# A hybrid decoder layer on one core: the front projections in three passes of rounded parts, the convolution's sums in PSUM, and a new tile order

## The chip, the cores and the metric

The kernel runs on one core of a Trainium2 chip. The metric is the device time of one execution in microseconds (us). In the text PE is TensorE (matrix products), DVE is VectorE, ACT is ScalarE, POOL is GpSimd and SP is SyncE, which here only issues transfers.

## The reference, cut to what matters

One layer for 256 prompt tokens and 8 sequences of 4 sample tokens, 288 tokens in all, with D_MODEL 1024:

```
h   = RMSNorm(x) * (1 + scale1) + shift1          # scale, shift, gate from silu(c) @ w_ada
h @ w_in -> q, k, v, indexer q, indexer k, indexer weights, conv input (a, g), gates A and B
branch A: the indexer picks top-k keys; softmax attention over them; @ w_o_attn
branch B: z = a * sigmoid(g); causal depthwise conv, width 31; LayerNorm; silu; @ w_conv_out
x += gate1 * ((sigmoid(gA) * A + sigmoid(gB) * B) @ w_out)
x += gate2 * PEER(RMSNorm(x) * (1 + scale2) + shift2)     # 16384 experts
```

The change lies in the front: `h @ w_in` without the gates, and the convolution. Everything from `w_conv_out` on keeps its products.

## The kernel before, in words

Activations are kept transposed: 128 channels on the partitions, 8 chunks `k`, 288 tokens along a row. A weight tile is 128x1024 float32 (512 KB) and gives 128 output channels for all tokens. SP streams the tiles in the order of `LOADS` through a ring of four slots: load n is issued when tile n-4 is done. `POS[key]` is a tile's place in that order, which `PLAN` sets by hand.

- The start: 16 `ada` tiles (four groups, `FIRST`) give scale1 and shift1. After two groups PE turns them (`mod_turned` 1), after all four again (`mod_turned` 2). DVE then makes `hT`, ACT and POOL make its rounded part and its remainder (`rhs_parts`, "h2r" in the profile).
- `HEAD`: 31 tiles (8 `conv_a`, 8 `conv_g`, `ki`, 4 `qi`, 2 `k`, 8 `q`), three `v` pieces whose weights lie in `v_w`, and 16 later `ada` tiles, one after each two of the others. `linear` (L1476) multiplies a tile straight from the ring as float32: 8 products that the profile shows as 16 records. ACT copies each result out of one of two PSUM banks `lin` (`evac`, or the sigmoid of L697). Beside that ACT loads the 16 pages of the key caches, two after each `conv_g` (`load_page`, L684).
- A tile of a stage in `STAGES` is cut instead (`CUT` is their list): ACT writes its part rounded to float32r (`cut_tile`, L667), POOL subtracts to get the remainder (`low_tiles`, L561), both into `split`, which has two slots; PE then does three passes of 8 products (`linear_cut`, L1513, L1519, L1525): high x high, high x low, low x high.
- The convolution is DVE's. For a pair of chunks it makes `z` (L1010, L1012), then 31 taps for each chunk by turns (L1019, L1023): 2 + 60 instructions of 128x256. The running sums stand in `y`, in SBUF. `conv_a` of chunk k goes to PSUM bank `pa[k % 4]`, so chunk k+4 waits for the `z` of chunk k. After the four pairs come the sample tokens: four times a product (L1033) and a reduction (L1036) of 128x1984, the "sample taps".
- The index stage (`for n in range(NQ * IH)`, 16 turns) follows the head: each second turn a `gate_a` tile and an `ada` tile, each turn an indexer head (PE L1633, relu L748 on ACT, L1063 on DVE), and from turn 3 on the QK norm's spread (L1641, L1070). Between them lie the LayerNorm's sums over `y` (L1457, after turn 6, waits for `y_sample`), the subtraction of the mean (L1076), ACT's square and the second sums (L1457, turn 12). Then come the sample indexer products (L1652), and a chain of DVE work (the top-k) up to the attention.

## Time and profile before

| | |
|---|---|
| median of 3 runs | 1407.49 us (1406.44 to 1407.97) |
| the profiled execution | 1407.39 us, its span 1405.6 us |
| PE busy | 1337.5 us (95%) |
| DVE, ACT, POOL busy | 976.6, 592.3, 767.8 us (69%, 42%, 55%) |
| mean granted TensorE clock | 0.976 |

The span is first to last instruction; 1.8 us of the time lie around it. A PE that is busy in 95% of the span counts the modelled ends of its instructions as well. A granted clock of 1.00 is 2.4 GHz and 0.50 is 1.2 GHz.

### The profile page before, as it was taken

What the parts mean: (1) busy time and instruction counts of PE and PEld (TensorE: products, weight loads), DVE (VectorE), ACT (ScalarE), POOL (GpSimd) and SP (SyncE); (2) the same over time, 40 slices, a digit from 0 to 9 for tenths busy, and PEclk for the clock granted to TensorE, in tenths of its full rate; (3) what the DMA queues carried; (4) which work ended last, traced back from release to release, by engine and by line L of the source; (5) the groups of instructions that cost most, each with busy time, mean ns of one, the idle gap of its engine ahead of it and who ended that gap; (6) DMA issues with size and microseconds to landing.
All of it is one profiled execution on the core that took longest, in us unless ns stands there. A gap on an engine that the chain in (4) does not pass through costs nothing.

```text
span 1405.6 us, 30010 instructions
## 1 busy us (share of the span) xinstructions
PE 1337.5 (95%) x9976; PEld 1253.2 (89%) x9976; DVE 976.6 (69%) x2130; ACT 592.3 (42%) x932; POOL 767.8 (55%) x335
## 2 busy tenths in 40 slices
PE   5999999889989999799999999999999999999996
PEld 3777677767879999789999999999999999999996
DVE  2499923965435999992666565650788888888886
ACT  1200234355434444554444444444444444444442
POOL 0200023520655477786655556557777777777774
PEclk8999999889998999999999999999999999999998
DMA  8776454234443456455545545456666666666663
GB/s 315 275 244 204 146 201 160 89 126 139 147 158 106 136 180 207 145 176 192 168 159 166 168 162 168 159 166 223 220 211 210 210 210 211 212 211 212 215 211 134
DMA packets 103750, 258.37 MB, mean 184 GB/s; under 512 B 12496, under 2 KB 52144, under 8 KB 103312
## 3 DMA queue, kind: packets, MB, share of 16 engines
q1 hardware_dynamic: 94144, 245.81, 52.0%
q10 hardware_dynamic: 8752, 8.93, 1.9%
q0 software_dynamic: 800, 2.91, 0.6%
q8 instruction: 33, 0.54, 0.2%
q14 instruction: 21, 0.17, 0.0%
HBM read 234.60 MB, written 23.00 MB: 183 GB/s over the span
## 4 chain that ended last, share of the span: by engine, by line
PE 87%; DVE 4%; issue 3%; POOL 2%; DMA 2%; ACT 1%; ACTq 0%; SPq 0%; POOLq 0%; DVEq 0%
PE ps L1868 28%; PE ps L1821 9%; PE ps L1476 9%; PE ps L1814 9%; PE ps L1815 8%; PE ps L1849 5%; PE ps L1513 4%; PE ps L1519 4%; PE ps L1525 3%; POOL split L596 2%; DMA ring<-in_stream 2%; PE ps L1536 1%; PE ps L1457 1%; PE ps L1799 1%; PE ps L1596 1%
## 5 line engine op out<-in xcount | busy, mean ns | idle before, releaser
L596 POOL TENSOR_TENSOR split<-ring,split 128x1024 fp32r<-128x1024 f32 x256 | 629.5, 2461 | 274.2 <-ACT split L869 274.0
L1868 PE MATMUL ps<-h2r,split 128*128 128x288 f32 x3072 | 406.4, 294 | 0.9 <-ACT h2r L931 0.9
L1868 PEld LDWEIGHTS ps<-h2r,split 128*128 128x128 f32 x3072 | 406.2, 188 | 1.1 <-ACT x L898 1.1
L869 ACT ACTIVATE split<-ring 128x1024 fp32r<-128x1024 f32 x256 | 270.4, 1057 | 205.7 <-PE ps L1868 204.1
L1436 DVE TENSOR_TENSOR h2r<-x,h2r 128x288 fp32r<-128x288 f32 x128 | 298.8, 2335 | 76.5 <-ACT h2r L931 76.5
L1814 PE MATMUL ps<-h2r,split 128*128 128x288 f32 x1024 | 284.9, 305 | 5.2 <-ACT split L869 5.2
L1815 PE MATMUL ps<-h2r,split 128*128 128x288 f32 x1024 | 278.8, 296 | 0.0
L561 POOL TENSOR_TENSOR split<-ring,split 128x1024 fp32r<-128x1024 f32 x48 | 118.7, 2475 | 179.1 <-ACT split L667 179.0
L1814 PEld LDWEIGHTS ps<-h2r,split 128*128 128x128 f32 x1024 | 193.9, 189 | 5.8 <-ACT split L869 3.8
L1815 PEld LDWEIGHTS ps<-h2r,split 128*128 128x128 f32 x1024 | 193.5, 189 | 0.0
L1821 PE MATMUL ps<-h2r,split 128*128 128x288 f32 x1024 | 165.3, 304 | 6.7 <-POOL split L596 6.4
L1821 PEld LDWEIGHTS ps<-h2r,split 128*128 128x128 f32 x1024 | 142.6, 190 | 9.8 <-POOL split L596 9.8
L898 ACT ACTIVATE x<-ps 128x288 f32<-128x288 f32 x124 | 51.1, 412 | 238.0 <-PE ps L1821 236.0
L1404 DVE TENSOR_SCALAR x<-ps,x 128x128 f32<-128x128 f32 x144 | 49.8, 346 | 117.3 <-PE ps L1849 107.2
L1476 PE MATMUL ps<-big,ring 128*128 128x288 f32 x496 | 127.2, 414 | 1.7 <-ACT mod L651 1.7
L1476 PEld LDWEIGHTS ps<-big,ring 128*128 128x128 f32 x496 | 93.5, 192 | 31.5 <-ACT big L657 2.9
L1405 DVE TENSOR_SCALAR x<-ps,x 128x128 f32<-128x128 f32 x288 | 115.5, 401 | 0.0
L1023 DVE SCALAR_TENSOR_TENSOR big<-big 128x256 f32<-128x256 f32 x240 | 95.3, 478 | 0.0
L1513 PE MATMUL ps<-h2r,split 128*128 128x288 f32 x448 | 79.6, 319 | 14.1 <-ACT split L667 5.5
L1513 PEld LDWEIGHTS ps<-h2r,split 128*128 128x128 f32 x448 | 66.8, 197 | 24.4 <-issue 16.4
L1519 PE MATMUL ps<-h2r,split 128*128 128x288 f32 x448 | 76.1, 309 | 0.0
L1427 DVE TENSOR_TENSOR x<-x,big 128x288 f32<-128x288 f32 x128 | 59.0, 461 | 20.3 <-DMA x<-act_dram 20.2
(240 smaller groups left out, 1349.1 us busy)
## 6 DMA issues: line engine op xcount, KB each, us to landing
ring<-in_stream SPq DMA_DIRECT2D x391, 512.0 KB, 3.3
act_dram<-x SPq DMA_DIRECT2D x128, 144.0 KB, 1.8
x<-act_dram SPq DMA_DIRECT2D x128, 144.0 KB, 3.0
big<-in_cache_k ACTq DMA_DIRECT2D x16, 128.0 KB, 3.3
big<-in_cache_v ACTq DMA_DIRECT2D x16, 128.0 KB, 3.2
x<-in_xT ACTq DMA_DIRECT2D x1, 1152.0 KB, 7.9
x_dram<-x ACTq DMA_DIRECT2D x1, 1152.0 KB, 5.2
big<-x_dram SPq DMA_DIRECT2D x1, 1152.0 KB, 5.0
```

The source lines that it names most:

```text
L561: nc.gpsimd.tensor_tensor(split[:, n % 2, 1], ring[:, POS[key] % R, :], split[:, n % 2, 0].bitcast(f32), ALU.subtract).then_inc(lin_lo, 1)
L596: nc.gpsimd.tensor_tensor(split[:, n % 2, 1], ring[:, slot_of(n), :], split[:, n % 2, 0].bitcast(f32), ALU.subtract).then_inc(lo_ready, 1)
L869: nc.scalar.activation(split[:, n % 2, 0], ring[:, slot_of(n), :], ACT.Copy).then_inc(hi_ready, 1)
L1405: return V.tensor_scalar(hot1[slot], iota_ps, parts[:, 0, col], parts[:, 2, col], ALU.is_equal, ALU.mult)
L1436: V.tensor_tensor(wr[:, n % 2, 1], act_b[:, n], wr[:, n % 2, 0].bitcast(f32), ALU.subtract)\
L1476: last = MM(bank[:, 0:T], w[:, k], rhs[:, k], start=(k == 0), stop=(k == KC - 1))
L1513: MM(out, hi[:, k], h_hi[:, k], start=(k == 0), stop=False)
L1519: last = MM(out, hi[:, k], h_lo[:, k], start=False, stop=False)
L1814: MM(out, u_hi[:, k], h_hi[:, k], start=(k == 0), stop=False)
L1815: last = MM(out, u_hi[:, k], h_lo[:, k], start=False, stop=False)
L1821: last = MM(out, u_lo[:, k], h_hi[:, k], start=False, stop=(k == KC - 1))
L1868: ins = MM(ps[k][:, 0:T], v[v_part][:, k], wr[:, n % 2, w_part], start=start, stop=stop)
```

## The change

- `STAGES[0]` takes the head's 31 tiles in: they are cut by ACT and POOL and multiplied by `linear_cut` in three passes; `linear` is gone. `rhs_lo` of `hT` is made in 8 chunks on POOL, and POOL cuts the head's remainders before it stores the convolution's state.
- The taps' running sums stand in the PSUM bank `pa[3]`; only the last tap writes `y`. `conv_a` has three banks left (`NCONV`).
- `HEAD`'s order: `ki` and `qi` after four chunks of the convolution, `v` and `k` before the last two chunks.
- Page loads move from ACT to SP: one page after each second tile load from load 24 on.
- `v_w`, `dist`, `causal` are issued at `mod_turned` 1 in place of 2.
- The sample taps move from behind the convolution into turns 1, 3, 5, 7 of the index stage; the sums over `y` move from turn 6 to 10, the subtraction from 7 to 11, the second sums from 12 to 14, ACT's `root(3)` behind the loop.

```diff
-HEAD = LINEAR[:LINEAR.index(("gate_a", 0))]
...
+HEAD = (CONV[:8] + [("ki", 0)] + [("qi", n) for n in range(4)] + CONV[8:12] + [("v", t) for t in range(NT)]
+        + [("k", n) for n in range(KV)] + CONV[12:] + [("q", n) for n in range(H)])
+NCONV = 3
...
-STAGES = [("gate_a", "gate_b"), ("conv_out",), ("attn_out",), ("out",), ("peer_q",)]
+STAGES = [("conv_a", "conv_g", "ki", "qi", "k", "q", "gate_a", "gate_b"), ("conv_out",), ("attn_out",), ("out",), ("peer_q",)]
...
+PAGES_AT = 24
...
+                page = (n - PAGES_AT) // 2
+                if n >= PAGES_AT and (n - PAGES_AT) % 2 == 0 and page < NSEQ * NPAGES:
+                    if page == 0:
+                        sp.wait_ge(pages_in, 16)
+                    load_page(page)
...
-            pool.wait_ge(mod_turned, 2)
+            pool.wait_ge(mod_turned, 1)
...
+            for k in range(KC):
+                pool.wait_ge(rhs_hi, k + 1)
+                nc.gpsimd.tensor_tensor(rhs_parts[:, 1, k * T:(k + 1) * T], hT[:, k],
+                                        rhs_parts[:, 0, k * T:(k + 1) * T].bitcast(f32), ALU.subtract).then_inc(rhs_lo, 1)
...
+            low_tiles(STAGES[0][:-2])
+            pool.wait_ge(conv_staged, 2)
...
+            cut_tile(CUT[0])
             cut_rhs(hT, h_ready, 3)
...
             for key in HEAD:
                 kind, m = key[:2]
+                if key in CUT:
+                    cut_tile(CUT[CUT.index(key) + 1])
...
-                        yp, w = y[:, k, 0:TP], wdw[:, k, j:j + 1]
+                        yp, w = pa[NCONV][:, k % 2 * TP:(k % 2 + 1) * TP], wdw[:, k, j:j + 1]
...
-                            ins = V.scalar_tensor_tensor(yp, zp[:, k, j:j + TP], w, yp, ALU.mult, ALU.add)
+                            ins = V.scalar_tensor_tensor(yp if j < CW - 1 else y[:, k, 0:TP], zp[:, k, j:j + TP], w, yp,
+                                                         ALU.mult, ALU.add)
...
-                if n == 7:
+                if n % 2 and n < 2 * TD:
+                    sample_taps(n // 2)
...
+                if n == 11:
...
-                    linear(key, hT, h_ready if key == ("conv_a", 0) else None)
+                    linear_cut(key)
...
-                if n == 6:
+                if n == 10:
```

SP's queue from its first row on, in the difference of the two programs. `ring<-in_stream` is a tile load, `pages` and `in_cache_...` belong to a page; the second page's rows repeat the first's.

```order
-L464 DMA ring<-in_stream 128x1024 x89
...
+L464 DMA ring<-in_stream 128x1024 x25
+L467 TENSOR_LOAD pages
+L467 ISA x2
+L470 ISA
+L470 DMA big<-in_cache_i 64x128 x2
+L470 ISA
+L470 DMA big<-in_cache_k 128x256
+L470 DMA big<-in_cache_v 128x256
+L464 DMA ring<-in_stream 128x1024 x2
```

Before, 89 tile loads stood in a row; now a page's rows stand behind load 24 and then behind each second load, sixteen times.

DVE before, from the last pair's taps to the first turns of the index stage (`big` holds `zp`, `y` and most other arrays, `ps` is PSUM):

```order
L1023 SCALAR_TENSOR_TENSOR big<-big 128x256 x60
L1033 TENSOR_TENSOR big<-big 128x1984
L1036 TENSOR_REDUCE big<-big 128x8x8
...
L1038 TENSOR_TENSOR big<-big 128x8x32
L1042 RECIPROCAL big<-big 10x288
L1049 TENSOR_TENSOR big<-big,ident 32x128 x2
L1060 TENSOR_SCALAR big<-big 128x128
```

And the same place now:

```order
L1024 SCALAR_TENSOR_TENSOR ps<-big,ps 128x256 x58
L1024 SCALAR_TENSOR_TENSOR big<-big,ps 128x256 x2
L1032 RECIPROCAL big<-big 10x288
L1053 TENSOR_SCALAR big<-big 128x128
L1056 SCALAR_TENSOR_TENSOR big<-big 128x128
L1040 TENSOR_TENSOR big<-big 128x1984
L1043 TENSOR_REDUCE big<-big 128x8x8
L1056 SCALAR_TENSOR_TENSOR big<-big 128x128 x2
L1063 SCALAR_TENSOR_TENSOR big<-big,ps 128x288
L1040 TENSOR_TENSOR big<-big 128x1984
L1043 TENSOR_REDUCE big<-big 128x8x8
```

The sample taps (a product and a reduction) stood ahead of the reciprocal and stand now inside the turns; the taps read and write PSUM.

POOL before, behind its first memsets, and then the same place now:

```order
L541 DMA big<-in_v_w 128x8x264
L546 TENSOR_TENSOR h2r<-big,h2r 128x2304
L550 DMA out_convpT<-big 128x240
L551 DMA out_convsT<-big 128x1920
L561 TENSOR_TENSOR split<-ring,split 128x1024 x8
```

```order
L552 DMA big<-in_v_w 128x8x264
L558 TENSOR_TENSOR h2r<-big,h2r 128x288 x8
L569 TENSOR_TENSOR split<-ring,split 128x1024 x31
L574 DMA out_convpT<-big 128x240
L575 DMA out_convsT<-big 128x1920
L569 TENSOR_TENSOR split<-ring,split 128x1024 x8
```

The one subtraction for `hT` became eight, and 31 remainders of head tiles stand behind them.

## Rows read from the trace of the kernel before

**Rows 1.** Two of the page's costliest groups: busy us, mean ns of one.

```profile
L869 ACT ACTIVATE split<-ring 128x1024 fp32r<-128x1024 f32 x256 | 270.4, 1057 | 205.7 <-PE ps L1868 204.1
...
L1023 DVE SCALAR_TENSOR_TENSOR big<-big 128x256 f32<-128x256 f32 x240 | 95.3, 478 | 0.0
```

**Rows 2.** The chain that ended last, the head's begin: start us, us, what.

```profile
38.92 9.14 PE ps L1476 x32
...
48.63 7.96 PE ps L1476 x32
```

**Rows 3.** The same chain where the head ends and a cut tile begins.

```profile
191.70 1.25 PE ps L1513 x8
...
195.07 0.57 PE ps L1536 x16
```

**Rows 4.** The same chain in the attn_out stage, cut tiles one after another.

```profile
363.06 1.07 PE ps L1513 x8
...
366.26 1.07 PE ps L1513 x8
```

**Rows 5.** Timeline in the head: start us, us, engine, line, operation, idle before.

```profile
97.22 0.99 PE L1476 MATMUL ps<-big,ring 128*128 128x288 f32 x3 [1.73 <-ACT mod L651]
```

**Rows 6.** Lines' own answers, POOL: duration ns min/median/max, first and last start.

```profile
L575 POOL TENSOR_TENSOR h2r<-big,h2r x8: 791/837/1007, 285.5 to 291.3; 128x288 fp32r<-128x288 f32 x8
...
L561 POOL TENSOR_TENSOR split<-ring,split x48: 2338/2397/4726, 188.2 to 484.2; 128x1024 fp32r<-128x1024 f32 x48
```

**Rows 7.** Timeline: PE turns two groups.

```profile
22.15 0.41 PE L1571 MATMUL ps<-ident,big 128*128 128x128 f32 x2 [1.04 <-ACT big L637]
```

**Rows 8.** Windows: us, busy of PE, PEld, DVE, ACT, POOL, granted clock, DMA share, GB/s.

```profile
24.00:36.00 12.00, 7.58 (x112) 4.30 (x112) 5.10 (x23) 0.28 (x1) 0.00 (x0) 0.52 0.99 381
```

**Rows 9.** Transfers issued from 40 to 192 us: KB each, median us to landing.

```profile
ring<-in_stream SPq DMA_DIRECT2D x47, 512.0 KB, 4.0
...
big<-in_v_w POOLq DMA_DIRECT2D x1, 1056.0 KB, 6.2
```

**Rows 10.** Timeline: two pages in a row on ACT's queue.

```profile
49.02 1.21 ACTq L684 DMA_DIRECT2D big<-in_cache_i  x2
...
52.08 1.13 ACTq L684 DMA_DIRECT2D big<-in_cache_i  x2
```

**Rows 11.** Timeline, DVE: the first sample taps, a product and a reduction.

```profile
158.25 2.22 DVE L1033 TENSOR_TENSOR big<-big 128x1984 f32<-128x1984 f32 x1
...
160.51 2.22 DVE L1036 TENSOR_REDUCE big<-big 128x64 f32<-128x1984 f32 x1
```

**Rows 12.** Timeline, the index stage: a DVE instruction beside POOL's.

```profile
201.06 2.38 POOL L561 TENSOR_TENSOR split<-ring,split 128x1024 fp32r<-128x1024 f32 x1 [5.79 <-ACT split L667]
...
201.58 2.47 DVE L1063 SCALAR_TENSOR_TENSOR big<-big 128x128 f32<-128x128 f32 x2 [0.63 <-ACT big L748]
```

**Rows 13.** Timeline, the out stage: DVE beside POOL, with PSUM operands.

```profile
392.50 0.48 DVE L1263 SCALAR_TENSOR_TENSOR x<-ps,mod,x 128x256 f32<-128x256 f32 x1 [2.38 <-PE ps L1525]
392.55 2.41 POOL L561 TENSOR_TENSOR split<-ring,split 128x1024 fp32r<-128x1024 f32 x1 [0.79 <-ACT split L667]
392.91 0.19 DVE L1265 TENSOR_TENSOR ps<-ps,mod 128x32 f32<-128x32 f32 x1
```

**Rows 14.** Lines' own answers, the index stage on DVE: ns min/median/max.

```profile
L1063 DVE SCALAR_TENSOR_TENSOR big<-big x14: 342/480/2010, 200.6 to 243.5; 128x128 f32<-128x128 f32 x7, 128x256 f32<-128x256 f32 x7
...
L1070 DVE SCALAR_TENSOR_TENSOR big<-big,ps x10: 499/505/514, 204.0 to 238.1; 128x288 f32<-128x288 f32 x10
```

**Rows 15.** Timeline, the index stage: DVE, ACT and PE.

```profile
198.01 1.94 DVE L1042 RECIPROCAL big<-big 10x288 f32<-10x288 f32 x1 [21.28 <-ACT big L726]
...
218.07 3.99 DVE L1076 TENSOR_TENSOR big<-big 128x2304 f32<-128x2304 f32 x1
...
222.10 2.13 ACT L615 ACTIVATE big<-big 128x2304 f32<-128x2304 f32 x1 [0.17 <-DVE big L1076]
...
243.21 4.17 PE L1652 MATMUL ps<-big 64*128 64x16 f32 x64 [0.74 <-ACT big L748]
```

More of the change, by code:

```diff
@@ L83, in spread @@
     return out
-HEAD = LINEAR[:LINEAR.index(("gate_a", 0))]
-HEAD.insert(HEAD.index(("k", 0)), ("v", 0))
-for t in range(1, NT):
-    HEAD.insert(HEAD.index(("v", t - 1)) + 1, ("v", t))
+HEAD = (CONV[:8] + [("ki", 0)] + [("qi", n) for n in range(4)] + CONV[8:12] + [("v", t) for t in range(NT)]
+        + [("k", n) for n in range(KV)] + CONV[12:] + [("q", n) for n in range(H)])
+NCONV = 3
 HEAD = spread(HEAD, 0, 16, 2)
@@ L464, in load, with load_page @@
                 sp.dma_start(ring[:, slot, :], a["stream"][n]).then_inc(tile_loaded[slot], 16)
+            def load_page(n):
+                page = sp.value_load(pages[0:1, n:n + 1], min_val=0, max_val=a["cache_k"].shape[0] - 1)
+                for dst, src in ((cache_i[0:ID, n], "cache_i"), (cache_i[ID:P, n], "cache_i"),
+                                 (cache_k[:, n].rearrange("p v n -> p (v n)"), "cache_k"), (cache_v[:, n], "cache_v")):
+                    sp.dma_start(dst, a[src][bass.ds(page, 1)].rearrange("o p n -> (o p) n")).then_inc(cache_in, 16)
             for n, at in enumerate(LOADS):
@@ L711, in _ @@
                 else:
-                    n = QK.index(key)
-                    if n == len(QK) - 1:
-                        cut_tile(("gate_a", 0))
                     evac(key, kT[:, m] if kind == "k" else q[:, m])
-                    evac(key, sq_qk[n], ACT.Square)
+                    evac(key, sq_qk[QK.index(key)], ACT.Square)
                     if key == ("q", 3):
@@ L749, in _ @@
                     .then_inc(idx_relu, 1)
+            root(3)
             eng.wait_ge(s_idx_prod, 1)
@@ L1027, in _, with sample_taps @@
                             ins.then_inc(y_prompt, 1)
+            dve.wait_ge(qk_root, 1)
+            V.reciprocal(qk_rms[0:len(QK)], qk_rms[0:len(QK)]).then_inc(qk_rstd, 1)
             samples = y[:, :, TP:T].rearrange("p k (b t) -> p k b t", t=TD)
-            for t in range(TD):
+            def sample_taps(t):
                 settle()
@@ L1076, in _ @@
                     V.tensor_tensor(y[:, :, :], y[:, :, :], over_chunks(rstd), ALU.subtract).then_inc(y_centred, 1)
+            dve.wait_ge(y_prompt, KC)
+            dve.wait_ge(y_sample, 1)
+            dve.wait_ge(conv_stored, 32)
+            wi = vtok[0:TS, NQ, KV * P:VW].rearrange("p (pair par) -> p par pair", par=2)
+            for par in range(2):
+                V.tensor_tensor(wi_diag[0:TS, par * 4:par * 4 + 4], wi[:, par].unsqueeze(2).to_broadcast([TS, 4, TS]),
+                                ident[0:TS, 0:TS].unsqueeze(1).to_broadcast([TS, 4, TS]), ALU.mult).then_inc(s_wi, 1)
             dve.wait_ge(idx_used, NQ * IH)
@@ L1458, in sums @@
                 return last
-            def linear(key, rhs, chunk_ready=None):
-                if key[0] == "conv_a":
-                    bank = pa[key[1] % 4]
-                    if key[1] >= 4:
-                        pe.wait_ge(z_ready, 2 * (key[1] - 4) + 2)
-                else:
-                    bank = lin[BANK[key]]
-                    free(BANKED.index(key))
-                pe.wait_ge(tile_loaded[POS[key] % R], 16 * (POS[key] // R + 1))
-                w = ring[:, POS[key] % R, :].rearrange("p (k m) -> p k m", m=P)
-                for k in range(KC):
-                    if chunk_ready is not None:
-                        pe.wait_ge(chunk_ready, 3 * k + 3)
-                    last = MM(bank[:, 0:T], w[:, k], rhs[:, k], start=(k == 0), stop=(k == KC - 1))
-                last.then_inc(tile_done, 1)
             def free(n):
@@ L1505, in linear_cut @@
                     if half == 0:
-                        free(BANKED.index(key))
+                        if key[0] == "conv_a":
+                            if key[1] >= NCONV:
+                                pe.wait_ge(z_ready, 2 * (key[1] - NCONV) + 2)
+                        else:
+                            free(BANKED.index(key))
                         pe.wait_ge(lin_hi, n + 1)
```

48 lines of the change are left out of this document (13 added, 35 removed).

## The prediction

> **What bounds the kernel now.** From the page I took that PE is busy in 95% of the span, so I looked at what the PE does in the front and at who would have to keep up with a faster PE. The chain that ended last runs through L1476, tile after tile, from 38.9 to 191.7 us [rows 2, 3]: the head is bound by PE. Two float32 tiles take 7.96 us [rows 2], 3.98 each, and with the ada tile behind them, 0.57 [rows 3], a pair takes 8.53. In all of it PE waited once, 1.73 us, for an ACT that was issuing page loads [rows 5]. Before the head PE waits for tile loads: from 24 to 36 us the DMA engines are 99% busy at 381 GB/s, and the granted clock is 0.52, near the 1.2 GHz level, while PE has gaps [rows 8]. Behind the head the index stage runs from 191.7 to the start of L1652 at 243.2 [rows 3, 15], 51.5 us, with a PE that hardly waits. The convolution ends on DVE at 158.3 and the sample taps follow it [rows 11], both hidden under the head.
>
> **The tiles: gain.** A cut tile that begins after other work takes from 191.70 to 195.07, 3.37 us [rows 3]; in a row they take 3.20 each [rows 4]. A head pair would be 3.37 + 3.20 + 0.57 = 7.14 us against 8.53: 0.70 us for each tile, and 31 tiles give **-21.7**. The page loads leave ACT, so its stall goes: **-1.7** [rows 5]. Bounds: -18 if each tile took 3.37 and the stall came back elsewhere, -24 if each took 3.20. ACT's cut of 1.06 [rows 1] and POOL's remainder of 2.40 [rows 6] come to 2.1 and 4.8 us in a pair of 7.14, so the PE covers them once they run ahead of it.
>
> **The first tiles: loss.** Float32 products needed only `hT`. Now ACT first cuts tile 0, then the 8 chunks of `hT`, and POOL makes 8 remainders of 0.84 us, as in L575 [rows 6], 6.7 in all. With the first chunk at about 39.5 they end at 46.2, tile 0's remainder at 48.6, its last pass (1.07 [rows 4]) at 49.7; tile 1's remainder at 51.0, PE at 52.1, ada at 52.7; tile 2's at 53.4, PE at 56.1; tile 3's cut stands on ACT behind the sigmoid of tile 1, so its remainder comes at 56.0, PE at 59.3, ada at 59.9. Before, that point was 57.2 [rows 2], and at the new pace it would be 54.4. The ramp costs **+5.5**. Bounds +4 (POOL a fifth quicker) and +9 (PE, with gaps, stays at the low clock through two tiles).
>
> **`v_w` earlier: loss.** `v_w`, `dist` and `causal` are 1056 [rows 9] + 128 + 128 KB, 1.34 MB. They used to start with `mod_turned` 2, when the head begins. Now they start at 22.6 [rows 7], into the stretch in which the DMA engines are full and PE waits for each tile. At 381 GB/s [rows 8] 1.34 MB are 3.5 us, by which the last ada tile, and the whole head, comes later: **+3.5**. Bounds 0 and +4.
>
> **Pages on SP: loss.** One page is 3.06 us of issuing on ACT's queue (49.02 to 52.08) [rows 10]; no row shows it on SP, and I take the same. Load n is issued when tile n-4 is done and lands 4.0 us later [rows 9]. Between lie 7.14 us, of which the cut wants 1.06: 2.1 to spare. Where a page follows the load of an ada tile, the next load is due 0.57 us later and is issued some 2.9 late, about 0.9 beyond what is spare. With pages behind each second load this comes once in six loads, five times in 32, less by slack at the `v` pieces: three to four times 0.9, **+3**. Bounds 0 (loads land in 3 us) and +8.
>
> **The convolution: nothing, by cover.** A DVE instruction with two SBUF inputs waits while POOL runs: at 201.58 two L1063 took 2.47 us, until POOL's of 201.06 had ended [rows 12]. With 31 remainders in the head the old form would meet that all along. With the sums in PSUM one SBUF tensor is left, and L1265 (one PSUM and one SBUF input, PSUM output) began 0.36 us into POOL's 2.41 and took 0.19 [rows 13]. Its length: 240 taps fill 95.3 us, 0.397 apart and 478 ns long [rows 1]; the nearest with a PSUM input and a pointer scalar, L1263, is 0.48 long [rows 13], so 0 to 0.02 more for each. It begins at 59.3 + 3.5 + 0.5 = 63.3, needs some 26 us for each of four pairs, waits for the late last `conv_g` at some 147 us, and ends near 174. It is wanted by the reciprocal of L1042, 6.3 us behind the head's end [rows 15], which is near 187 now. So 13 us are spare; spacing decides only above 0.49 us a tap.
>
> The Trainium skill, "VectorE: DVE Perf Modes", section "The TRN2 errata — SBUF-src ops pay a fixed extra latency per instruction", gives VectorE a fixed 120 cycles from PSUM against 58 from SBUF. By that estimate a tap would be 0.065 us longer (15.6 us over 240) and the convolution would end some 12 us later than I have it, just covered; the rows here show a fifth of that or less.
>
> **Sample taps in the index stage: loss.** They are 2.22 + 2.22 us four times [rows 11], 18 us that the head hid. In turns 1 to 7 DVE has for each two turns 4.5 of taps and some 1.6 of its own (two L1063, two L1070 [rows 14]), and the product has two SBUF inputs, so it collides with POOL's remainders, say 0.5 each: 6.6 us. PE has (51.5 less two sums of 4.0) / 8 = 5.4, and it waits for DVE through the spread (`qk_ready`), two turns behind. Four rounds: 4 x 1.2 = 4.8. The subtraction and the square, 4.0 + 2.1 [rows 15], now have only turns 11 to 14 over them in place of 7 to 12: 0.7 more. PE's lead of two turns gives back about half a round, 2.5. **+3**. Bounds 0 and +8 (each collision in full, 2.4). `root(3)` and `wi_diag` fill waits of ACT and DVE under L1652's 4.2 us [rows 15]; what follows is unchanged.
>
> **Sum.** -21.7 - 1.7 + 5.5 + 3.5 + 3 + 3 = -8.4. Against the profiled execution's own 1407.4 us, which is the median within 0.1, that is **1399.0 us**. Under 0.2% (2.8 us, so above 1404.7) is about what can't be told from no change.
>
> **The rivals.**
> *The losses are covered.* SP issues a page more quickly or loads land in 3 us, and the taps find more room than I see: then ramp and `v_w` alone count, -14.4: 1393.0; with `v_w` hidden too, 1389.5. For it: DVE is idle between the convolution's end and the first turns. Against: 6.6 us in two turns are plain sums of rows. Chance 0.22.
> *The clock eats the gain.* In the ramp and the index stage PE gets gaps, and it had 0.52 where it had gaps before [rows 8]. Four tiles at 1.2 GHz would be 13 us longer, half of it under waits already counted: -8.4 + 6.5, 1405.5. Against: at 191.7 a pass still took 1.07 us as in the full stream [rows 4]. Chance 0.13.
> *SP becomes the bound* (the slower side). Two loads want 0.8 us of SP and PE takes 4.8 for two loads. Above 4.0 us a page SP sets the pace, and each microsecond more costs 16. At 4.5 the gain is gone (+8); at 4.9 it is -8.4 + 14.4 = +6, 1413.4. For it: no row shows a page on SP. Against: 3.06 on ACT [rows 10]. Chance 0.10.
> *The taps wait for POOL after all.* Pointer scalar and chunk both lie in SBUF; if that counts as two inputs, 31 remainders of 2.4 us block DVE for 74 us, the convolution ends near 248, 61 beyond its cover: 1460. Against: [rows 13]. Chance 0.04.
>
> **How the numbers follow.** The forecast holds 0.51; its own range, by half of the bounds, is 1394 to 1404. The range over all takes in the covered case and most of the clock's: **1389 to 1407**; SP's bound and the blocked taps lie outside. Faster by over 0.2%: 0.51 x 0.98 + 0.22 + 0.13 x 0.25 = 0.75. Within: the rest of the clock's case and the edges, 0.11. Slower: 0.10 + 0.04 = 0.14.
>
> **What would show it.** Cut tiles of 3.2 to 3.4 us in the head; the head's first product near 42.4 instead of 38.9; the fourth tile done near 63 instead of 56.6; waits of ACT or PE in the head for `ring`, three to five of about 0.9 us; the head's end near 180; taps 0.40 to 0.42 apart; an index stage of 54 to 55 us in which PE waits for DVE. I am wrong if the start doesn't move, if SP's queue has no waits for tiles left (SP bound), if taps stand over 0.49 apart, or if the granted clock is near 0.50 behind 50 us.

## The result: no gain, 0.27% slower

The changed kernel took 1411.2 us (median of 12 runs, 1406.11 to 1414.61) against 1407.2 us (12 runs, 1404.97 to 1409.85): ratio 1.0027, 95% interval 1.0015 to 1.0038. The forecast was 1399.0 us; the time lies outside the range and on the other side of no change. Where a number below is "before" without a group, it is from the trace of the kernel before.

The page of the changed kernel, whose profiled execution took 1412.23 us:

```profile
span 1410.4 us, 30634 instructions
...
PE 1330.5 (94%) x10224; PEld 1271.4 (90%) x10224; DVE 983.6 (70%) x2130; ACT 623.1 (44%) x963; POOL 844.8 (60%) x373
```

PE is 7.0 us less busy than before, and the span is 4.8 us longer: the products did become cheaper, and gaps took 11.8 us, more than they saved. Read at five points of the two traces (us from the span's start):

| | before | changed | difference | forecast |
|---|---|---|---|---|
| head's first product | 38.7 | 42.3 | +3.6 | +3.5 |
| fifth tile starts | 57.1 | 65.0 | +7.9 | +6.3 |
| head's end | 191.7 | 186.8 | -4.9 | -11.4 |
| sample indexer products | 243.2 | 244.0 | +0.8 | -8.4 |
| span | 1405.6 | 1410.4 | +4.8 | -8.4 |

The first row is the start in the timeline of both kernels; the 38.9 of the prediction is the same product in the chain of [rows 2].

**The head's begin.** Timelines of PE (start us, us, engine, line, operation, idle before), the second turning of the `ada` results in the kernel before and in the changed one, then the first cut product:

```profile
38.26 0.66 PE L1571 MATMUL ps<-ident,big 128*128 128x128 f32 x2 [0.49 <-ACT big L637]
```

```profile
40.19 0.66 PE L1565 MATMUL ps<-ident,big 128*128 128x128 f32 x2 [0.49 <-ACT big L649]
```

```profile
42.26 1.85 PE L1507 MATMUL ps<-h2r,split 128*128 128x288 f32 x5 [1.40 <-ACT h2r L686]
```

The first turning began at 22.15 before [rows 7] and begins at 21.91 now, so between the two lie 18.3 us in place of 16.1: the `ada` tiles come 2.2 us later behind the earlier `v_w`. From the second turning to the first product it is 2.07 us in place of 0.45, because a cut product also waits for ACT's rounded `hT`.

The chain that ended last (start us, us, what), where [rows 2] show the kernel before:

```profile
49.14 2.34 POOL split L569
...
51.52 2.29 PE ps L1519 x8
53.81 1.49 PE ps L1507 x8
...
57.38 0.57 PE ps L1530 x16
```

POOL's remainder of tile 0 is ready at 51.5, 0.6 earlier than summed (48.6 + 3.5). But the pass that waits for it takes 2.29 us in place of 1.07, and the next 1.49. The windows say why (columns as in [rows 8]):

```profile
40.00:50.00 10.00, 5.41 (x16) 3.98 (x17) 6.82 (x16) 5.84 (x12) 7.20 (x9) 0.50 0.35 126
50.00:60.00 10.00, 9.32 (x68) 8.61 (x68) 0.52 (x2) 4.61 (x5) 7.33 (x4) 0.77 0.30 97
```

PE was busy 5.4 of the 10 us from 40 on, with gaps, and the granted clock stood at 0.50, the 1.2 GHz level; before, with PE busy without a gap, it was 0.92 there. The first two tiles end 1.8 us later than summed.

DVE and POOL in the same stretch (timelines):

```profile
41.67 0.41 DVE L999 TENSOR_SCALAR big<-big,scl,mod 128x256 f32<-128x256 f32 x1
...
42.20 0.95 DVE L999 TENSOR_SCALAR big<-big,scl,mod 128x256 f32<-128x256 f32 x1
...
43.79 0.83 DVE L998 TENSOR_TENSOR big<-big,scl 128x32 f32<-128x32 f32 x1
```

```profile
42.20 5.54 POOL L558 TENSOR_TENSOR h2r<-big,h2r 128x288 fp32r<-128x288 f32 x7 [17.55 <-ACT h2r L686]
```

As soon as POOL begins its remainders of `hT`, DVE's instructions that write the next chunks of `hT` take two to five times as long (before: 0.40 and 0.18). I had only thought of ACT and POOL there.

**The middle of the head.** The chain where the SP queue issues a page; L464 is a tile's load, L467 the page number's register, L470 the page's transfers:

```profile
68.44 3.83 DMA ring<-in_stream
...
79.33 1.08 PE ps L1519 x8
...
80.43 0.34 SPq L464
...
80.81 0.27 SPq L467
...
84.05 0.38 SPq L470
...
84.48 3.99 DMA ring<-in_stream
...
88.49 1.06 ACT split L679
...
89.69 1.29 PE ps L1507 x8
...
99.99 5.08 DMA ring<-in_stream
```

A tile is done at 80.41 and one load is issued; behind it stands a page, from 80.81 to 84.43 (3.6 us). The next load is due at 80.97, when the `ada` tile is done, and is issued only at 84.48. It lands 3.99 later, is cut in 1.06, and PE starts at 89.69, having waited 0.86. Such a load comes once in six, as forecast: those of 68.44, 84.48 and 99.99 are issued 3.3, 3.5 and 2.7 us late (forecast 2.9). The page shown is one of the long ones. The sixteen pages on SP take 2.93 to 3.97 us each in this trace, median 2.94, so the price taken, 3.06, was right. PE by lines from 65 to 122 us (last column: idle before, and for whom):

```profile
L1507 PE MATMUL ps<-h2r,split 128*128 128x288 f32 x104 | 16.5, 301 | 4.2 <-ACT split L679 3.7 <-ACT big L669 0.5
```

Seven pairs with their `ada` tiles lie between 65.03 and 121.68, 8.09 us each, not 7.14 (one of the fourteen is a `v` piece). In stretches of two pairs, each with one late load: from 65.03 to 81.33, to 97.81 and to 113.71 it is 16.30, 16.48 and 15.90 us, where e3 below takes 14.30 (72.56 to 86.86). A late load thus costs 1.6 to 2.2 us, though PE's wait for it is 0.86 to 1.24, as forecast: the pair behind it waits as well (0.36 at 81.33, 0.53 at 97.81).

**The index stage.** Chain at the head's end, then timelines of DVE, POOL and PE; before: [rows 3, 11, 12, 15]:

```profile
186.79 1.26 PE ps L1507 x8
...
193.12 1.92 DVE big L1032
```

```profile
197.99 2.22 DVE L1043 TENSOR_REDUCE big<-big 128x64 f32<-128x1984 f32 x1
200.13 3.02 DVE L1056 SCALAR_TENSOR_TENSOR big<-big 128x128 f32<-128x128 f32 x2
```

```profile
196.16 6.38 POOL L569 TENSOR_TENSOR split<-ring,split 128x1024 fp32r<-128x1024 f32 x2 [5.79 <-ACT split L679]
```

```profile
244.00 2.20 PE L1646 MATMUL ps<-big 64*128 64x16 f32 x34 [0.74 <-ACT big L748]
```

Two remainders of 2.4 us take 6.38 beside DVE's sample taps, and DVE's L1056 then 3.02 for two (before 0.35 each where POOL was idle). From 186.8 to 244.0 the stage takes 57.2 us against 51.5. PE waits only 2.0 us in it:

```profile
L1519 PE MATMUL ps<-h2r,split 128*128 128x288 f32 x66 | 10.8, 305 | 1.1 <-POOL split L569 1.1
...
L1635 PE MATMUL ps<-big,ident 10*128 10x288 f32 x20 | 6.9, 439 | 0.9 <-DVE big L1063 0.9
```

In this trace the rest is in the passes: in this stretch, by the same view, one record of L1507 and L1513 takes 328 and 332 ns, and of the same two passes before (L1513, L1519) 308 and 295; the granted clock was 0.83, 0.92 and 0.90 in the three stretches of 10 us from 200 on, and 1.00 in all of them before. But the lower clock is not what makes the stage long. e3 (below) has the same code in this stage; its windows row:

```profile
180.40:237.00 56.60, 51.57 (x409) 40.40 (x408) 37.65 (x37) 21.82 (x42) 22.82 (x12) 1.00 0.51 182
```

With the clock at 1.00 throughout, its stage takes 56.6 us all the same. PE waits 4.3 us in it in place of 2.0, and DVE is busy for 37.7 us as in the changed kernel, against 19.4 before. So the work on DVE sets the length (e10 takes part of it away), and PE spends the time in waits or in slow passes.

**The convolution.** DVE's timeline, 58 taps of a pair:

```profile
66.54 22.81 DVE L1024 SCALAR_TENSOR_TENSOR ps<-big,ps 128x256 f32<-128x256 f32 x58
```

22.81 / 58 is 0.393 us a tap, beside a POOL that cuts a tile every 3.5 us; before it was 0.397 [rows 1] with POOL idle.

### The profile page after: what moved, and what is told of

The parts are those of the page before. It is cut to its first block, busy times and chain, and to the rows that moved or that the text cites. A ratio compares the mean times of both kernels' runs of the same rounds, so it can differ in the third digit from the quotient of the medians.

```text
span 1410.4 us, 30634 instructions
## 1 busy us (share of the span) xinstructions
PE 1330.5 (94%) x10224; PEld 1271.4 (90%) x10224; DVE 983.6 (70%) x2130; ACT 623.1 (44%) x963; POOL 844.8 (60%) x373
## 4 chain that ended last, share of the span: by engine, by line
PE 81%; DVE 6%; issue 4%; DMA 4%; POOL 2%; ACT 2%; SPq 1%; POOLq 0%; ACTq 0%; DVEq 0%
PE ps L1862 28%; PE ps L1815 9%; PE ps L1808 8%; PE ps L1809 8%; PE ps L1507 6%; PE ps L1513 5%; PE ps L1519 5%; PE ps L1843 5%; DMA ring<-in_stream 3%; POOL split L608 2%; PE ps L1530 1%; PE ps L1465 1%; PE ps L1793 1%; DVE big L1132 1%; PE ps L1590 1%
## 5 line engine op out<-in xcount | busy, mean ns | idle before, releaser
L608 POOL TENSOR_TENSOR split<-ring,split 128x1024 fp32r<-128x1024 f32 x256 | 628.9, 2458 | 273.8 <-ACT split L870 273.7
L1862 PE MATMUL ps<-h2r,split 128*128 128x288 f32 x3072 | 406.4, 294 | 0.9 <-ACT h2r L932 0.9
L1862 PEld LDWEIGHTS ps<-h2r,split 128*128 128x128 f32 x3072 | 406.2, 188 | 1.1 <-ACT x L899 1.1
L870 ACT ACTIVATE split<-ring 128x1024 fp32r<-128x1024 f32 x256 | 270.4, 1056 | 205.8 <-PE ps L1862 202.7
L569 POOL TENSOR_TENSOR split<-ring,split 128x1024 fp32r<-128x1024 f32 x79 | 194.1, 2464 | 234.1 <-ACT split L679 221.7
L1808 PE MATMUL ps<-h2r,split 128*128 128x288 f32 x1024 | 285.1, 306 | 5.2 <-ACT split L870 5.2
L1809 PE MATMUL ps<-h2r,split 128*128 128x288 f32 x1024 | 278.7, 296 | 0.0
L1808 PEld LDWEIGHTS ps<-h2r,split 128*128 128x128 f32 x1024 | 194.0, 189 | 5.8 <-ACT split L870 3.8
L1809 PEld LDWEIGHTS ps<-h2r,split 128*128 128x128 f32 x1024 | 193.7, 189 | 0.0
L1815 PE MATMUL ps<-h2r,split 128*128 128x288 f32 x1024 | 164.9, 303 | 5.6 <-POOL split L608 5.2
L1815 PEld LDWEIGHTS ps<-h2r,split 128*128 128x128 f32 x1024 | 142.3, 189 | 8.9 <-POOL split L608 8.9
L1507 PE MATMUL ps<-h2r,split 128*128 128x288 f32 x696 | 124.7, 322 | 23.7 <-ACT split L679 10.2
L1507 PEld LDWEIGHTS ps<-h2r,split 128*128 128x128 f32 x696 | 105.0, 200 | 40.6 <-issue 23.7
L1412 DVE TENSOR_SCALAR x<-ps,x 128x128 f32<-128x128 f32 x144 | 49.8, 346 | 113.9 <-PE ps L1843 107.2
L679 ACT ACTIVATE split<-ring 128x1024 fp32r<-128x1024 f32 x87 | 91.8, 1055 | 83.0 <-DMA ring<-in_stream 56.4
L1513 PE MATMUL ps<-h2r,split 128*128 128x288 f32 x696 | 118.5, 314 | 0.0
L1519 PE MATMUL ps<-h2r,split 128*128 128x288 f32 x696 | 111.2, 303 | 1.9 <-POOL split L569 1.8
L1513 PEld LDWEIGHTS ps<-h2r,split 128*128 128x128 f32 x696 | 106.2, 202 | 1.6 <-DVE h2r L1244 0.2
L1519 PEld LDWEIGHTS ps<-h2r,split 128*128 128x128 f32 x696 | 101.3, 196 | 3.8 <-POOL split L569 3.7
```

What stands on the lines that cost most here:

```text
L569: nc.gpsimd.tensor_tensor(split[:, n % 2, 1], ring[:, POS[key] % R, :], split[:, n % 2, 0].bitcast(f32), ALU.subtract).then_inc(lin_lo, 1)
L608: nc.gpsimd.tensor_tensor(split[:, n % 2, 1], ring[:, slot_of(n), :], split[:, n % 2, 0].bitcast(f32), ALU.subtract).then_inc(lo_ready, 1)
L870: nc.scalar.activation(split[:, n % 2, 0], ring[:, slot_of(n), :], ACT.Copy).then_inc(hi_ready, 1)
L1507: MM(out, hi[:, k], h_hi[:, k], start=(k == 0), stop=False)
L1513: last = MM(out, hi[:, k], h_lo[:, k], start=False, stop=False)
L1519: last = MM(out, lo[:, k], h_hi[:, k], start=False, stop=(k == KC - 1))
```

## The experiments

All are built from the changed kernel unless said otherwise, and timed in 5 rounds (e4 in 3) against the kernel before on the same chip. "Head's end" is the start of the first `gate_a` tile. Where two experiments are compared, their medians are subtracted as they stand; the kernel before had 1407.2 to 1408.5 in the sessions, so up to 1.3 us of such a difference can be the session's. A trace is of one execution: that of e2 took 7.1 us more than e2's median and that of e5 5.0 less than e5's, the others lie within 2.5 of theirs.

### e1: v_w later

```diff
-            pool.wait_ge(mod_turned, 1)
+            pool.wait_ge(mod_turned, 2)
```

> The changed kernel with v_w, dist and causal issued at mod_turned 2 again. My theory (their 1.34 MB delay the last ada tiles): the head's first cut product comes at 38.9 us instead of 42.3, the head ends near 183.4 instead of 186.8, and the time is 3.4 us less than the changed kernel's, about 1.000 of the kernel before. Rival (the load only moves its cost: at 40 us it delays the head's own tiles, whose landing is now tight): the start comes 3.4 earlier, but the head's end moves by less than 1.5 us and the time by less than 1.5.

Measured: 1410.6 us (12 runs), ratio 1.0019 (1.0002 to 1.0035). The first product came at 39.5, 2.7 earlier; the third tile at 57.47, 0.4 earlier; the head's end at 188.2. POOL's timeline:

```profile
39.22 0.94 POOL L552 DMA_DIRECT2D big<-in_v_w  x1 [36.35 <-PE ps L1565]
...
41.32 4.60 POOL L558 TENSOR_TENSOR h2r<-big,h2r 128x288 fp32r<-128x288 f32 x6
```

The 2.7 us were won and lost within 10 us: POOL now issues three transfers for 2.0 us at the moment when `hT` wants its remainders, which then run in a row. Beside them one DVE instruction that writes `hT` takes 3.15 us (from 41.27) in place of 0.18, and PE waits 3.46 us before its product at 44.94. e8 and e9 take this apart.

### e2: the sample taps ahead of the reciprocal

All four steps, the sums over `y` and the subtraction back in the turns of before:

```diff
+            for t in range(TD):
+                sample_taps(t)
+            settle()
+            V.tensor_tensor(y[:, :, TP:T], ...).then_inc(y_sample, 1)
             dve.wait_ge(qk_root, 1)
             V.reciprocal(...)
```

> The changed kernel with the sample taps, the sums over y, the subtraction, the squares and root(3) where they were before. My theory (DVE sets the pace of the index stage): the stage, from the head's end to the sample indexer products, takes 51.5 to 55 us instead of 57.2, not the full 51.5, since the taps now end near 197 and the reciprocal of the QK norm stands behind them, some 3 us late; time 2 to 4 us less. Rival (the low clock after the head and collisions of POOL with DVE made the stage long, whatever DVE holds): 56 us or more, time within 1 us of the changed kernel's.

Measured: 1413.5 us (9 runs), ratio 1.0036 (1.0021 to 1.0051). DVE's timeline, the first step's product and the reciprocal:

```profile
184.15 3.27 DVE L1037 TENSOR_TENSOR big<-big 128x1984 f32<-128x1984 f32 x1
...
205.75 1.93 DVE L1048 RECIPROCAL big<-big 10x288 f32<-10x288 f32 x1
```

The expectation missed. The prompt's convolution ends at 184, so the eight instructions run until 205.4 and the reciprocal comes 13.0 us behind the head's end (192.8) in place of 6.3. PE waits 5.5 us for it, and the stage takes 59.6 us, where 51.5 to 55 were expected. That the head ends 6 us later than in the changed kernel's trace is not the edit's doing, for the sample taps begin only at 184: this execution was the slowest of its nine. The kernel before has cover for all four steps (its convolution ends at 158); here 8.7 us lie between the convolution's end and the head's, about two steps. e10 tries that.

### e3: pages behind every third load

Each page follows the load that stands in front of an `ada` tile's. The load behind the page is then due 3.2 us later, one tile, and not 0.57:

```diff
-PAGES_AT = 24
+PAGE_AFTER = [n for n in range(20, len(LOADS) - 1) if ("ada",) ==
+              tuple(key[0] for key, p in POS.items() if p == n + 1)][:NSEQ * NPAGES]
...
-                page = (n - PAGES_AT) // 2
-                if n >= PAGES_AT and (n - PAGES_AT) % 2 == 0 and page < NSEQ * NPAGES:
+                if n in PAGE_AFTER:
```

> The changed kernel with a page behind the tile load that stands in front of an ada load (each third load) instead of each second load. My theory (SP's queue issues tile loads late, 3.6 us a page): pairs of head tiles take 7.2 to 7.4 us instead of 8.1, the head ends at 180 to 182 instead of 186.8, time 5 to 6 us less. Rival (the DMA engines' rate or the depth of the ring bounds the supply, whoever issues and when): pairs stay at 7.9 or more and the head ends less than 2 us earlier.

Measured: 1403.1 us (11 runs), ratio 0.9964 (0.9953 to 0.9976), 8 us below the changed kernel. PE by lines, 65 to 122 us, beside the changed kernel's row above:

```profile
L1507 PE MATMUL ps<-h2r,split 128*128 128x288 f32 x104 | 16.6, 301 | 0.5 <-ACT split L679 0.5
```

The idle time before L1507 falls from 4.2 to 0.5 us; a pair takes 7.15 us (72.56 to 79.71) and the head ends at 180.4, 6.4 earlier. The sixteen pages cost SP what they did (median 2.94 us), only their places differ. That settles the SP term. The time fell by 8 us where 5 to 6 were expected and the head gives 6.4; the rest is open.

### e4: the sums back in SBUF

```diff
-                        yp, w = pa[NCONV][:, k % 2 * TP:(k % 2 + 1) * TP], wdw[:, k, j:j + 1]
+                        yp, w = y[:, k, 0:TP], wdw[:, k, j:j + 1]
```

> The changed kernel with the convolution's running sums in SBUF again. My theory (two SBUF inputs wait while POOL subtracts): DVE taps that meet one of POOL's remainders take up to 2.8 us, the convolution ends 50 to 75 us later and becomes the bound; the time is 40 to 70 us more, 1.03 to 1.05 of before. Rival (a single wait per remainder with DVE catching up between, or POOL waiting for DVE as often): under 20 us more, with POOL's remainders lengthened to over 3 us.

Measured: 1489.9 us (4 runs), ratio 1.0572 (1.0550 to 1.0593). L1024's own answer (ns min/median/max, first and last start):

```profile
L1024 DVE SCALAR_TENSOR_TENSOR big<-big x240: 467/470/2618, 71.5 to 240.6; 128x256 f32<-128x256 f32 x120
```

The taps' median has not moved, and yet they last 169 us in place of 111. Timelines of DVE and POOL, and PE by lines from 60 to 245 us, show where the time is:

```profile
71.47 23.83 DVE L1024 SCALAR_TENSOR_TENSOR big<-big 128x256 f32<-128x256 f32 x60
```

```profile
75.50 24.33 POOL L569 TENSOR_TENSOR split<-ring,split 128x1024 fp32r<-128x1024 f32 x2 [4.11 <-ACT split L679]
```

```profile
L1519 PE MATMUL ps<-h2r,split 128*128 128x288 f32 x191 | 33.8, 325 | 71.6 <-POOL split L569 71.5
```

It is not so much DVE that is held as POOL: two taps of 240 took 2.6 us, but 60 run in 23.8 us as ever, one behind the other, and the remainder that POOL begins at 75.50 gets through only when they are over (it took 22.0 us; three others took 19.5 to 21.7). PE waits 71.5 us for such remainders, and the late `conv_g` tiles then leave DVE idle. The expectation had 40 to 70 us and the wrong engine. So the bank in PSUM is worth 79 us here, by keeping DVE's stream out of POOL's way.

### e5: the first four tiles whole

Tiles 0 to 3 are multiplied as float32 straight from the ring (the old `linear`), and ACT cuts from the fifth on:

```diff
+WHOLE = CONV[:4]
-CUT = [key for key in PLAN if any(key[0] in kinds for kinds in STAGES)]
+CUT = [key for key in PLAN if any(key[0] in kinds for kinds in STAGES) and key not in WHOLE]
...
-                    linear_cut(key)
+                    if key in WHOLE:
+                        linear(key, hT, h_ready if key == ("conv_a", 0) else None)
+                    else:
+                        linear_cut(key)
```

> The changed kernel, but its first four tiles are multiplied whole as float32 products, as in the kernel before; only the other head tiles and all later ones are cut. The output is the reference's. Theory (the ramp costs more than it gives: cut products there wait for GpSimd's low halves of hT, which collide with VectorE's own instructions on hT): the fourth tile and its ada products are done near 60.6 us, that is the 57.2 of the kernel before plus the 3.4 by which the first product starts later, in place of 65.1; from there the pairs take the same 8.1 us, so the head ends near 182.3 in place of 186.8 and the time is about 4 us below the changed kernel's. Rival (the SP queue is late with every ring tile from 20 on and sets the end of the head by itself): the ring's loads don't start earlier, the gain of 4.5 us is used up waiting for the ring before the pages are all issued, and the time is within 1 us of the changed kernel's.

Measured: 1404.8 us (12 runs), ratio 0.9975 (0.9961 to 0.9989). The fifth tile starts at 60.53 and the head ends at 182.58, both as expected; the time is 6 us below the changed kernel's, 2 more than expected. The ring waits stay, as the theory has it, and merely begin earlier:

```profile
69.30 0.90 PE L1528 MATMUL ps<-h2r,split 128*128 128x288 f32 x5 [1.53 <-ACT split L680]
```

### e6: the kernel before with v_w early

The kernel before, its `pool.wait_ge(mod_turned, 2)` made a 1.

> The kernel before with one edit of the change alone: the load of v_w and of the two mask tensors is let go at mod_turned 1 in place of 2. The output is the reference's. My prediction priced this at +3.5 us, since the 1056 KB then stand ahead of adaLN's tiles in the same 381 GB/s. Theory as predicted: first product 3 to 3.5 us later than 38.9, nothing gives it back, and the time 3 us up. Rival (as it went in the changed kernel, where letting it go later moved the first product by 2.8 us but the third tile by 0.4): the third tile starts within 1 us of 48.6 and the time doesn't move. The rival would need a wait other than the adaLN tiles there, and the kernel before has none on GpSimd, so I hold with the first, 70 to 30.

Measured: 1409.1 us (12 runs) against 1408.5 (23 runs), ratio 1.0006 (0.9995 to 1.0017). In its trace the first product is 2.7 us later, the head's end 3.1, the sample indexer products 3.1, the span 1.8. So each profile has the 3 us, and the medians have 0.6, at most 2.4 by the interval. I can't reconcile the two from one profile of each. What is steady over the traces is the stretch between the two turnings: 17.8 to 18.3 us in the nine with `v_w` early, 16.0 to 16.2 in four of the five with it late and 14.8 in the fifth (e9).

### e7: e5 and e3 together

> The changed kernel with two edits: the first four tiles whole as float32 products, and the pages' loads put out by the sync engine after every third load, so that each falls behind a tile that is not of the pairs. The output is the reference's. Theory (the two losses add up, since one lies ahead of 65 us and the other behind it): the fourth tile is done near 60.6 us, pairs of about 7.15 us, head end near 175.9 (180.4 with the pages alone moved, less 4.5), time 4 us below the 1403 of the kernel with only the pages moved, that is near 1399. Rival (with the pairs this short the ring's transfers, not the queue, are the next limit, or the granted clock falls further): the head ends at 178 or later and the time stays at 1402 to 1404.

Measured: 1397.3 us (6 runs), ratio 0.9924 (0.9907 to 0.9940). Fifth tile at 58.78, head's end at 173.69, both about 2 us earlier than expected; but its first turning was already at 20.2 (22.3 in e5), before any edit acts, so these 2 us are this execution's and not the edits'. By the medians the gains are 8.1 (e3), 6.4 (e5) and 13.9 for both. The two losses add.

### e8: e7 with v_w later

> The kernel of the two edits (first four tiles whole, pages after every third load), and v_w with the masks let go at mod_turned 2 as in the kernel before. The output is the reference's. Theory: the late v_w gained 2.8 us at the first product of the changed kernel and lost it again because GpSimd's low halves of hT then ran over VectorE's instructions; with whole products nothing waits for these halves until the fifth tile, so the 2.8 to 3.4 us stay: fourth tile done near 57.5, head end near 172.7, time near 1396. Rival: the collision slows VectorE's writing of hT itself, which the whole products need too, so that the first tile ends as late as with v_w early, and the time is that of the kernel with two edits, within 1 us.

Measured: 1400.9 us (6 runs), ratio 0.9942 (0.9919 to 0.9964). PE's and DVE's timelines:

```profile
38.87 3.76 PE L1504 MATMUL ps<-big,ring 128*128 128x288 f32 x10
44.65 1.33 PE L1504 MATMUL ps<-big,ring 128*128 128x288 f32 x2 [2.02 <-DVE big L1004]
```

```profile
41.44 3.15 DVE L1004 TENSOR_TENSOR big<-big,mod 128x32 f32<-128x32 f32 x1
```

The rival held. The remainders of `hT`, piled up behind POOL's three issues, run one after another from 41.49, and a DVE instruction of 0.18 us takes 3.15. PE, on whole tiles, waits for `hT` itself.

### e9: POOL holds the remainders back

```diff
+            pool.wait_ge(h_ready, 3 * KC)
             for k in range(KC):
                 pool.wait_ge(rhs_hi, k + 1)
```

> The kernel with whole first four tiles, pages after every third load and v_w let go late (first product 38.9, fourth tile done 63.0, 1400.9 us), with one line more: GpSimd waits for the last of VectorE's instructions on hT before it takes the low halves of hT. The output is the reference's. Theory (what ate the 2.8 us of the late v_w was GpSimd's subtractions piled up behind its three DMA issues, which held one VectorE instruction for 3.15 us): VectorE's instructions on hT take 0.4 and 0.18 us again, TensorE has no wait of 2.02 us, the fourth tile is done near 57.5, head end near 172.7, time near 1395. Rival (the stall of VectorE comes from the 1056 KB load's descriptors being written by GpSimd, whose issues end at 41.4, just when the long instruction begins, not from the subtractions): the instruction at 41.4 stays near 3 us long, the fourth tile is done near 62 to 63, time near 1400.

Measured: 1394.2 us (5 runs), ratio 0.9905 (0.9893 to 0.9918). DVE's and POOL's timelines:

```profile
40.02 0.18 DVE L1001 TENSOR_TENSOR big<-big,scl 128x32 f32<-128x32 f32 x1
40.12 0.40 DVE L1002 TENSOR_SCALAR big<-big,scl,mod 128x256 f32<-128x256 f32 x1
```

```profile
37.88 0.94 POOL L553 DMA_DIRECT2D big<-in_v_w  x1 [35.01 <-PE ps L1587]
...
40.71 6.14 POOL L560 TENSOR_TENSOR h2r<-big,h2r 128x288 fp32r<-128x288 f32 x8 [0.82 <-DVE big L1005]
```

The subtractions were the cause, not the issues: with the same three issues in the same place DVE is back at 0.18 and 0.40. The fifth tile starts at 56.94, the head ends at 171.97, and the time is 6.7 us below e8's, from which it differs by this one line, and 3.1 below e7's.

### e10: two sample steps ahead

e7 with two of the four steps before the reciprocal:

```diff
+            AHEAD = 2
+            for t in range(AHEAD):
+                sample_taps(t)
             dve.wait_ge(qk_root, 1)
...
-                if n % 2 and n < 2 * TD:
+                if n % 2 and 2 * AHEAD < n < 2 * TD:
```

> The kernel with whole first four tiles and pages after every third load (1397.3 us), with two of the four steps of the sample taps moved back ahead of the reciprocal, into the 14.8 us in which VectorE waits for the root. The output is the reference's. In the kernel before all four lie in the head and its index stage takes 51.5 us; here it takes 57.2, and the steps fill VectorE to 99% from 182 to 208 us. Theory (the +5.7 us are VectorE's time in that stage and GpSimd's waits behind it): half of the 17.8 us leaves the stage, it takes 54 to 55 us, and the time falls by 2 to 3. Rival (as when all four were moved: GpSimd's low halves of the last head tiles wait behind the steps, so TensorE waits there): the head ends 2 us later or more and the time is the same or up.

Measured: 1392.0 us (6 runs), ratio 0.9892 (0.9875 to 0.9908), 5.2 below e7. DVE's timeline, the last reduction of the two steps and the reciprocal:

```profile
175.28 2.22 DVE L1041 TENSOR_REDUCE big<-big 128x64 f32<-128x1984 f32 x1
182.42 1.94 DVE L1047 RECIPROCAL big<-big 10x288 f32<-10x288 f32 x1 [4.91 <-ACT big L730]
```

The two steps end at 177.5, 4.9 us before the reciprocal's input is there, and the index stage takes 51.6 us (176.03 to 227.60), what it took before the change, where 54 to 55 were expected; in e7 it takes 57.2. PE has no wait for DVE or POOL left in it.

### e11: pages back on ACT

The changed kernel with the pages where the kernel before has them, two behind the sigmoid of each `conv_g`: eight sigmoids, not the four that the expectation names.

> The changed kernel with the pages' loads put back exactly where the kernel before has them, on ScalarE after each of the first four Sigmoids. The output is the reference's. Theory (the whole of the SP term was 8 us, as the kernel with the pages spread out showed): ScalarE's stall of 1.7 us comes back, tiles from 65 to 122 us take about 7.15 us a pair in place of 8.09, less the hold-ups where ScalarE issues 8 DMAs before it can cut the next tile (4 times about 4 us of ScalarE's time, of which it has slack), head end near 181 to 183, time near 1405. Rival: ScalarE is now the engine that cuts every tile, so the issues, 8 to a tile, delay the cuts by their whole time and the head ends at 186 or later, as in the changed kernel, time 1410.

Measured: 1442.8 us (5 runs), ratio 1.0250 (1.0229 to 1.0270). Both sides of the expectation missed. ACT's and PE's timelines:

```profile
78.91 2.01 ACT L674 ACTIVATE split<-ring 128x1024 fp32r<-128x1024 f32 x2 [5.66 <-issue]
```

```profile
80.11 2.26 PE L1512 MATMUL ps<-h2r,split 128*128 128x288 f32 x8 [3.34 <-ACT split L674]
```

The cut that stands behind two pages: ACT is kept from cutting for 5.7 us. PE waits 3.3 to 5.1 us behind seven of the eight sigmoids, and behind six of these waits its next pass takes 2.2 to 2.3 us, the lower clock level again (1.34 behind the seventh). The head ends at 222.8, 36 us later. With ACT cutting every tile the pages could not stay there.

### e12: all mends together

e9 and e10 in one kernel.

> All the mends that worked, together: first four tiles whole as float32 products, v_w and masks let go late, GpSimd's low halves of hT after VectorE's last instruction on hT, pages after every third load on the sync engine, two of the four steps of the sample taps ahead of the reciprocal. The output is the reference's. Theory (the losses lie in different stretches, so the mends add): fourth tile done near 57, head end near 173, index stage 51.7 us, so the samples' index products start near 225 (227.6 with the taps' edit alone), time 1389 to 1390, 1.25% below the kernel before. Rival (an edge moved earlier at the start is given back behind it, as it seemed in the kernel before, where v_w early moved every stage by 3 us and the time by 0.6): time 1391 to 1393.

Measured: 1388.6 us (4 runs), ratio 0.9863 (0.9844 to 0.9882): 19.2 us below the kernel before. The chain, where [rows 2] have the head's begin:

```profile
48.10 7.96 PE ps L1507 x32
...
56.63 1.25 PE ps L1531 x8
```

Head's end at 171.0, sample indexer products at 222.6, 20.6 before those of the kernel before.

## Why the prediction was wrong

**The sum failed by too small losses, each of the kind that it names.** The steps that failed most are the 0.9 us for each late load behind a page (+3, measured +6.6) and the sample taps in the index stage (+3, measured +5.7). Its terms against what was measured:

| term | forecast | measured | by |
|---|---|---|---|
| cut tiles | -21.7 | -20.4 | e3: 115.2 us from the fifth tile to the head's end; the terms give 113.9 |
| ACT's stall | -1.7 | -1.7 | no wait for a page on ACT left |
| `v_w` earlier | +3.5 | +3.6 | first product 42.3 against 38.7; only 2.2 of it is the `ada` tiles' delay |
| first tiles | +5.5 | +7.0 | fifth tile at 65.0, less 3.6, against 54.4 |
| pages on SP | +3 | +6.6 | head's end 186.8 against the 180.2 that the other terms give; e3 takes off 6.4 |
| taps in the index stage | +3 | +5.7 | 57.2 against 51.5; e10 gives 51.6 |
| convolution in PSUM | 0 | 0 | 0.393 us a tap; e4 |

They come to +0.8, the difference at the sample indexer products. Forecast and profiled span lie 13.2 us apart (-8.4 against +4.8): 9.2 up to that point and 4.0 behind it.

**Pages on SP** is the largest miss, 3.6 us. The page's price was right (median 2.94 us on SP, 3.06 taken), so was the place where it hurts, behind the load of an `ada` tile, and so was the count, once in six loads. What failed is the 0.9 us for each: that is the wait of the tile whose load is late (0.86 to 1.24), but the pair behind it is late too, and two pairs lose 1.6 to 2.2 us together. I took a late load as an event by itself. The rival "SP becomes the bound" was set to decide only from 4.5 us a page, by an average over six loads; what counts is the queue's state when the next load is due. e3, with the same pages at the same price in better places, is free of it.

**The first tiles**: POOL's sum came out right to 0.6 us. The 1.5 us more are the bound that I named and did not take, PE with gaps at the lower clock level: the granted clock was 0.50 from 40 to 50 us and 0.77 from 50 to 60, so the rival "the clock eats the gain" was at work here, for less than it priced. e5 with e7 shows that the better plan was to leave these four tiles whole: cutting pays 0.70 us a tile and cost 7.0 before it paid.

**Taps in the index stage**: the mechanism, DVE's 17.8 us and the collisions with POOL's remainders, was in the sum and its size was not. The changed kernel's granted clock of 0.83 to 0.92 from 200 to 230 us (before 1.00) looks like a further cause, but e3's stage takes 56.6 us with 1.00 throughout. Two steps of the sum rested on no row. Each collision was put at 0.5 us, and the two long ones on DVE cost 2.3 (3.02 for two at 200.13) and 1.7 (2.04 for one at 214.54). PE's lead was to give back 2.5, and without that the sum has 5.5, near the measured 5.7. No run separates the two. e10 shows that moving half the taps away gives all of it back.

**`v_w` earlier**: that the first product moved by 3.6 us where 3.5 were forecast is luck in good part. The `ada` tiles lost 2.2 us, not 3.5, and 1.6 more are the wait of a cut product for ACT's rounded `hT`, which belongs to the first tiles. What a later `v_w` gives back depends on POOL: nothing in e1 and a loss in e8. In e9 against e7 it is 3.1 us and in e12 against e10 3.5, but both also hold POOL's remainders of `hT` back, and no run does that with `v_w` early, so the two parts aren't separated. In the kernel before (e6) the medians show at most 2.4.

**"What follows is unchanged"**: behind the sample indexer products the profiled run is 4.0 us longer (1166.4 against 1162.4). The other traces, which share this code, have from 1159.5 (e5) to 1166.4 (e2) there, with no order by edit, so I take most of the 4.0 for scatter. The medians differ by 3.8 to 4.0 all the same, where the terms give 0.8; the 3 us between stay open.

**Right**: the length of a cut tile, the price of a page, the convolution with its sums in PSUM and its cover (DVE waits 14.8 us for the reciprocal's input, 13 were forecast). The rival of the blocked taps had a fair price (61 us more; e4 took 79) and the wrong victim: with the sums in SBUF it is POOL that the taps block, and hardly they that POOL blocks. On the section of the Trainium skill quoted in the prediction ("VectorE: DVE Perf Modes", the fixed cost from PSUM): 0.393 us a tap from PSUM against 0.397 from SBUF shows none of the 0.065 us that its figures would add to a tap. (What the rows of the prediction allowed, 0 to 0.02, is up to a third of that, not a fifth.)

**Not priced**: that leaving the pages on ACT would have cost 32 us (e11). I booked the move as 1.7 us won against 3 lost; its real alternative was the kernel of e11.

## What to carry to other kernels

When an engine's work per tile falls, price each queue at the moment when its next item is due, not on average, and follow a late item to the next one: 3 us of page issues are harmless in one place of a three-load round and cost about 1 us a round in another. Start a cheaper but longer pipeline (cut, remainder, three passes) only once its buffers are full, and run the first tiles in the plain form. And ask of every work that leaves its cover (sample taps) or stays where it was (pages on ACT) how much cover is left with the new pace: half of the taps fitted, all did not.

## What the runs showed of the hardware that I had not expected

- A DVE instruction with one SBUF tensor and two scalars read by pointer is held by POOL too: L999 took 0.95 us beside POOL's subtraction and 0.41 alone; one of 0.18 us with two inputs took 3.15 beside subtractions in a row (e8). With the running sum in PSUM no tap was held, though its scalar is read by pointer as well (longest 486 ns).
- The hold works both ways, and in both kinds of case seen here the engine with the dense stream wins: two remainders of POOL took 6.38 us beside DVE's 128x1984 product (4.76 in the head, beside taps with their sums in PSUM), and one took 22.0 us behind 60 taps in a row (e4).
- After six gaps of 3.3 to 5.1 us PE's next pass took 2.17 to 2.29 us; in the one of 80.11 the passes were back at 1.23 within the same pair (e11). Such a gap costs more than its own length. One gap of 3.7 us left the pass at 1.34, so it does not always do so.
- The time of one kernel moves loosely with the mean granted clock of its run: of the 12 runs of the changed kernel the fastest took 1406.1 us at 0.973, the one with the lowest clock 1412.2 at 0.963, and the slowest 1414.6 at 0.967.
